# Running ten gate products inside the attention of a kernel's last two layers, with fused bias and maximum

## What is computed

```python
n = rms_norm(h, norm_g[i, 1])
(aq, ak, av, bq, ..., cq, ck, cv, ga, gb, gc) = split_cols(n @ w_in[i], IN_SPLITS)
ya = diff_attention(...)      # 4 heads x 2 parts, causal
yb = nsa_attention(...)       # 8 heads x 3 branches (compressed, selected, window)
yc = swa_sink_attention(...)  # 8 heads, softmax with a sink
merged = (jax.nn.sigmoid(ga) * (ya @ w_branch[i, 0])
          + jax.nn.sigmoid(gb) * (yb @ w_branch[i, 1])
          + jax.nn.sigmoid(gc) * (yc @ w_branch[i, 2]))
h = h + merged @ w_out[i]
```

## Time and profile before

| | us |
|---|---|
| median of three runs | 4402.25 |
| the profiled execution | 4387.95 |
| its span in the trace | 4386.1 |
| attention stage, layer 0 and 1 | 85 and 85 |
| gates stage, layer 0 and 1 | 74 and 73 |

### The profile page before, as it was taken

The page is one execution under the profiler, slowest core; times in us unless marked ns, Lnnn a source line. Parts: engine busy times, 40 slices in busy tenths (PEclk is TensorE's granted clock), DMA queues, the critical chain, the costliest instruction groups (busy, mean ns, idle before and its releaser), DMA issues. The chain is left out here.

```text
span 4386.1 us, 74092 instructions
## 1 busy us (share of the span) xinstructions
PE 4025.2 (92%) x28216; PEld 3843.6 (88%) x28216; DVE 3287.4 (75%) x5784; ACT 2041.9 (47%) x3503; POOL 1184.7 (27%) x1023
## 2 busy tenths in 40 slices
PE   7887988999999998979999999799899989989898
PEld 5666988999999997669999999698788989978897
DVE  6886898778688887668977788666667676667766
ACT  5253334767433334345444444444654454456444
POOL 0000002667688892110188455000000000000000
PEclk9998999999999998989999999899999999989999
DMA  7332445998999995346866888454244545433453
GB/s 254 105 131 101 143 154 181 330 333 293 318 337 333 333 334 193 136 142 204 276 226 217 280 297 300 156 185 162 68 133 161 186 153 186 162 101 101 161 185 124
DMA packets 281605, 896.15 MB, mean 204 GB/s; under 512 B 29424, under 2 KB 73424, under 8 KB 278822
## 3 DMA queue, kind: packets, MB, share of 16 engines
q1 hardware_dynamic: 223286, 673.80, 45.6%
q0 software_dynamic: 55520, 201.60, 13.6%
q10 hardware_dynamic: 2448, 16.02, 0.9%
HBM read 834.92 MB, written 56.14 MB: 203 GB/s over the span
## 5 line engine op out<-in xcount | busy, mean ns | idle before, releaser
L153 DVE TENSOR_TENSOR weight_lo<-weight_ring,weight_hi 128x1024 fp32r<-128x1024 f32 x1084 | 1356.7, 1252 | 633.5 <-ACT weight_hi L148 617.0
L148 ACT ACTIVATE weight_hi<-weight_ring 128x1024 fp32r<-128x1024 f32 x1084 | 1142.6, 1054 | 1210.9 <-issue 706.8
L185 PE MATMUL pair0e_acc<-pair_xh,weight_hi 128*128 128x384 f32 (+1 forms) x1152 | 407.9, 354 | 12.6 <-ACT pair0e_gelu L2679 10.6
L185 PE MATMUL pair0e_acc<-pair_xl,weight_hi 128*128 128x384 f32 (+1 forms) x1152 | 397.0, 345 | 0.0
L185 PE MATMUL pair0e_acc<-pair_xh,weight_lo 128*128 128x384 f32 (+1 forms) x1152 | 396.4, 344 | 0.0
L185 PE MATMUL pair0e_acc<-pair0e_coef_hi,weight_hi 128*128 128x384 f32 x1024 | 343.2, 335 | 9.5 <-DVE pair0e_coef_lo L2391 9.5
L185 PE MATMUL pair0e_acc<-pair0e_coef_lo,weight_hi 128*128 128x384 f32 x1024 | 342.9, 335 | 0.0
L185 PE MATMUL pair0e_acc<-pair0e_coef_hi,weight_lo 128*128 128x384 f32 x1024 | 342.8, 335 | 0.0
L185 PE MATMUL peer10e_dot<-peer_xh,weight_hi 128*128 128x224 f32 (+1 forms) x1152 | 324.8, 282 | 8.2 <-DVE weight_lo L153 6.6
L185 PE MATMUL peer10e_dot<-peer_xh,weight_lo 128*128 128x224 f32 (+1 forms) x1152 | 317.5, 276 | 0.0
L185 PE MATMUL peer10e_dot<-peer_xl,weight_hi 128*128 128x224 f32 (+1 forms) x1152 | 317.4, 276 | 0.0
(11 more groups left out here) (632 smaller groups left out, 12367.1 us busy)
## 6 DMA issues: line engine op xcount, KB each, us to landing
weight_ring<-in_w_tiles SPq DMA_DIRECT2D x572, 512.0 KB
weight_ring<-in_peer_tiles SPq DMA_DIRECT2D x512, 512.0 KB
pair_acts<-pair0e_gelu SPq DMA_DIRECT2D x64, 384.0 KB
pair0e_act_in<-pair_acts SPq DMA_DIRECT2D x64, 384.0 KB
peer_acts<-peer10e_gelu SPq DMA_DIRECT2D x64, 224.0 KB
peer10e_act_in<-peer_acts SPq DMA_DIRECT2D x64, 224.0 KB
pair_coefs<-pair0e_G ACTq DMA_DIRECT2D x12, 1024.0 KB, 14.1
pair0e_kept_in<-pair_coefs SPq DMA_DIRECT2D x64, 192.0 KB
```

What stands on the lines that cost most here:

```text
L148: act.activation(self.tile_of(self.hi, g), self.ring[:, g % RING, :], ACT.Copy).then_inc(self.hi_done, 2)
L153: dve.tensor_tensor(self.tile_of(self.lo, g), self.ring[:, g % RING, :], self.tile_of(self.hi, g).bitcast(F32), ALU.subtract).then_inc(sel ...
L185: last = pe.matmul(out, lhsT, rhs, start=start and i == 0, stop=stop and i == len(passes) - 1, **more)
```

## The change

Of the 24 gate tiles the first ten (`GATES_IN`) are now used inside attention, by a new function `biased_attention` that replaces `attention` in the second block. `GateJobs` does half a tile in each of the 20 steps, on PE behind the scores. All ten use one PSUM bank, `gate_acc`; VectorE scales its sum into `sig` in every second step. ScalarE and VectorE convert the weight tiles there too. The gates stage does the other 14, and ScalarE does the sigmoids of the first ten in it as well. On VectorE the bias and the maximum become one `tensor_tensor_reduce`, which scales by 1/8 after the addition, so the bias table is made 8 times as large. The four results of a step share one PSUM bank: PE waits before a step's first output matmul for all earlier results to be copied, and ScalarE waits for the whole step before it copies them. `sig` now exists during attention; the memory of X_hi and X_lo, not needed by then, lies over it.

```diff
+GATES_IN = 10
...
-            ("ffn1_", 3 * FC), ("in_cols", 21), ("in_rows", 8), ("cmp", 9), ("gates", 24), ("branch", 12),
+            ("ffn1_", 3 * FC), ("in_cols", 21), ("in_rows", 8), ("cmp", 9), ("gates_in", GATES_IN), ("gates", 24 - GATES_IN), ("branch", 12),
...
-        act.activation(self.at(c), self.at(c), ACT.Sigmoid)
+        act.activation(self.at(self.done + c), self.at(self.done + c), ACT.Sigmoid)
+        if c < self.done:
+            act.activation(self.at(c), self.at(c), ACT.Sigmoid)
...
+class GateJobs:
+
+
+    def __init__(self, W, first, x, sig, by_token):
+        self.W, self.first, self.x, self.sig, self.by_token = W, first, x, sig, by_token
+
+    def open(self, S):
+        self.acc = S.ps("gate_acc", [P, 512])
+        self.read = S.sem("gate_read")
+        self.owed = self.W.take_owed()
+        self.kept = 2 * (self.first + GATES_IN) - 1
+        self.W.owed = self.kept
+
+    def feed(self, sync):
+        self.W.feed(sync, self.first, GATES_IN)
+
+    def half(self, pe, n):
+
+        c, half = divmod(n, 2)
+        if c >= GATES_IN:
+            return
+        part = 2 * self.first + n
+        self.W.wait(pe, part)
+        if half == 0 and c:
+            pe.wait_ge(self.read, c)
+        for i in range(4):
+            k = 4 * half + i
+            last = run_passes(pe, self.acc[:, 0:T], self.W.stationary(part, i * P, self.x(k)), k == 0, k == KD - 1)
+        last.then_inc(self.W.used, 1)
+
+    def scale(self, dve, c):
+        if 0 <= c < GATES_IN:
+            dve.wait_ge(self.W.used, 2 * (self.first + c) + 2)
+            dve.tensor_tensor(self.sig[:, c // 8, c % 8, :], self.acc[:, 0:T], self.by_token, ALU.mult).then_inc(self.read, 1)
+
+    def high(self, act, c):
+        if 0 <= c < GATES_IN - 1:
+            self.W.next_hi(act, 2 * (self.first + c) + 1)
+
+    def low(self, dve, c):
+        if 0 <= c < GATES_IN - 1:
+            self.W.next_lo(dve, 2 * (self.first + c) + 1)
...
+def biased_attention(nc, name, units, ident, fill):
...
+        out = S.ps("out", [P, 4, P])
...
+            scores(0)
+            for s in range(steps + 2):
+                scores(s + 1)
+                fill.half(pe, s)
+                for u, i, x in batch(s - 1):
+                    pe.wait_ge(normed, u + 1)
+                    if i % H == 0 and s >= 2:
+                        pe.wait_ge(copied, u - B + H)
+                    for b in range(x.nk // P):
+                        last = pe.transpose(turned[:, i, b * P:(b + 1) * P], prob[:, (s - 1) % 2, i, b * P:(b + 1) * P], ident)
+                    last.then_inc(transposed, 1)
+                for u, i, x in batch(s - 2):
+                    pe.wait_ge(copied, u + 1)
+                    if i == 0 and ends_before(s - 2):
+                        pe.wait_ge(evacuated, ends_before(s - 2))
+                    nb = x.nk // P
+                    for b in range(nb):
+                        last = pe.matmul(out[:, group[u] % 4, :], x.v(b), probT[:, s % 2, i, b * P:(b + 1) * P],
+                                         start=(x.first and b == 0), stop=(x.end and b == nb - 1), skip_group_check=True)
+                    last.then_inc(summed, 1)
...
+            if fill.owed is not None:
+                fill.W.next_lo(dve, fill.owed)
+            for s in range(steps + 1):
+
+                now, b = batch(s), s % 2
+                if now:
+                    dve.wait_ge(scored, s + 1)
+                    for u, i, x in now:
+                        last = dve.tensor_tensor_reduce(biased[:, b, i, 0:x.nk], raw[:, b, place(i), 0:x.nk], x.bias,
+                                                        x.scale, NEG, ALU.add, ALU.max, low[:, b, i:i + 1])
+                    chain(last)
...
+                if s % 2:
+                    fill.scale(dve, (s - 3) // 2)
...
+                if s % 2:
+                    fill.low(dve, (s - 3) // 2)
+            for c in range((steps - 1) // 2, GATES_IN):
+                fill.scale(dve, c)
+                fill.low(dve, c)
...
+                if s % 2:
+                    fill.high(act, (s - 3) // 2)
...
+                done = batch(s - 2)
+                if done:
+                    act.wait_ge(summed, (s - 1) * B)
+                for u, i, x in done:
+                    if x.end:
+                        lo, hi, dst = x.out
+                        act.activation(dst, out[lo:hi, group[u] % 4, :], ACT.Copy).then_inc(evacuated, 1)
...
-                act.activation(bias[:, 2 * n:2 * n + 2, :], acc[:, n % 4, :, :], ACT.Copy).then_inc(copied, 1)
+                act.activation(bias[:, 2 * n:2 * n + 2, :], acc[:, n % 4, :, :], ACT.Copy, scale=8.0).then_inc(copied, 1)
...
-                attention(nc, "attn", units, ident)
+                biased_attention(nc, "attn", units, ident, GateJobs(W, W.take("gates_in" + n), x, sig, in_rstd[:, 0:T]))
...
-            products(nc, W, "gates", first, 24, column_jobs(W, first, 24, KD, T, x),
-                     lambda dve, chain, c, ps: dve.tensor_tensor(sig[:, c // 8, c % 8, :], ps[:, 0:T], in_rstd[:, 0:T], ALU.mult),
-                     "vector", follow=Sigmoids(lambda c: sig[:, c // 8, c % 8, :],
+            def gate(c):
+                return sig[:, c // 8, c % 8, :]
+
+            products(nc, W, "gates", first, 24 - GATES_IN, column_jobs(W, first, 24 - GATES_IN, KD, T, x),
+                     lambda dve, chain, c, ps: dve.tensor_tensor(gate(GATES_IN + c), ps[:, 0:T], in_rstd[:, 0:T], ALU.mult),
+                     "vector", follow=Sigmoids(gate, GATES_IN,
```

More of the change, by code:

```diff
@@ L786, with __init__ @@
 class Sigmoids(Follow):
-    def __init__(self, at, more):
-        self.at, self.more = at, more
+    def __init__(self, at, done, more):
+        self.at, self.done, self.more = at, done, more
     def open(self, S, ready):
@@ L3576, in second_layer @@
             y = tmp_sb("y", [P, 3, 4, T])
+            sig_at = -(-nc.sbuf_base // 32) * 32
+            sig = tmp_sb("sig", [P, 3, KD, T])
             with ExitStack() as attn:
@@ L3582, in second_layer @@
                 X = at_sb("X", [P, 2, 3, XT])
-                X_hi, X_lo = at_sb("X_hi", [P, 11, XT], F32R), at_sb("X_lo", [P, 11, XT], F32R)
+                X_hi, X_lo = (nc.alloc_sbuf_tensor_at("second%d_X_%s" % (layer, part), [P, 11, XT], F32R,
+                                                      offset=sig_at + i * 4 * 11 * XT) for i, part in enumerate(("hi", "lo")))
                 av = at_sb("av", [P, 2, 512])
@@ L3655, in second_layer @@
                                 out=(64 * g, 64 * g + 64, y[half, 2, r, tt * P:(tt + 1) * P])))
-                attention(nc, "attn", units, ident)
+                biased_attention(nc, "attn", units, ident, GateJobs(W, W.take("gates_in" + n), x, sig, in_rstd[:, 0:T]))
             at = col_at("subln") + layer
             y_hi, y_lo = tmp_sb("y_hi", [P, 3, 4, T], F32R), tmp_sb("y_lo", [P, 3, 4, T], F32R)
-            sig = tmp_sb("sig", [P, 3, KD, T])
             term = tmp_sb("term", [P, 2, T])
             first = W.take("gates" + n)
-            products(nc, W, "gates", first, 24, column_jobs(W, first, 24, KD, T, x),
-                     lambda dve, chain, c, ps: dve.tensor_tensor(sig[:, c // 8, c % 8, :], ps[:, 0:T], in_rstd[:, 0:T], ALU.mult),
-                     "vector", follow=Sigmoids(lambda c: sig[:, c // 8, c % 8, :],
+            def gate(c):
[3 more added lines that the diff above has]
+                     "vector", follow=Sigmoids(gate, GATES_IN,
                                                HeadNorm(y, y_hi, y_lo, ones, cols[:, at:at + 1],
@@ L3853, in layout_weights @@
         f["cmp" + n] = np.concatenate([w1, padded_tile(w2)])
-        f["gates" + n] = column_tiles(w[:, 3608:])
+        gate_tiles = column_tiles(w[:, 3608:])
+        f["gates_in" + n], f["gates" + n] = gate_tiles[:GATES_IN], gate_tiles[GATES_IN:]
         wb = a["w_branch_2"][i]
```

87 lines of the change are left out of this document (added).

## The result

The changed kernel takes 4438.42 us (median of five runs, 4428.3 to 4442.33), the kernel before 4407.09 in five runs beside it. The ratio is 1.0086, with an interval of 1.0067 to 1.0105: **slower by 0.9%**. The prediction had +24 us and the right sign. The time lies inside its range, above its middle.

A forecast was written before the change was run, and what follows sets the result against it. PE was taken to become attention's bound: 68.6 + 30.4 + 19 + 6 = 124.0 us against 84.5, +39.5; gates -27.4; net +12.1 a layer, +24 for two. Forecast 4426 us (+0.55%), range 4396 to 4450.

The forecast's parts named there:

- point 7: Start and end of attention: 6 us a layer for the start, its lower clock and the end.
- a rival of 12%: Attention: PE's clock drops again and again behind its pauses, 15 us a layer, 4456 us in all; chance 12%.
- PE's own work: Attention on PE without waits: 68.6 us a layer, plus 30.4 for the half products, 99.0 in all.
- Points 1 and 5: Gates stage loses ten tiles, gain 27.4 us a layer; ScalarE's added weight and copy work in attention priced at 0.
- the first rival: Attention: gate-bank waits cost next to nothing and matmul forms change for free, 94.6 us a layer, 4368 in all; chance 14%.
- Point 3: Attention, single gate bank: PE waits nine times a layer for VectorE's read, 19 us, with 0.9 more in each sink step.
- Point 4: Fused bias and maximum on VectorE: 0.21 us at 128 columns, 0.34 at 256; its saving worthless except inside gate-bank waits.
- The third rival: Attention on VectorE: the fused form takes 0.29 us instead of 0.21, 4 us a layer, 4434 in all; chance 16%.
- Point 6: Attention, one bank for a step's four results: removes PE waits of 1.1 us.
- The sign's turning point: The whole change turns from faster to slower where attention lasts 112 us, nine waits of 1.0 us on top of 103.

The follow-up runs named there:

- read_first: Changed kernel with VectorE's read of the gate bank moved ahead of its wait for the step's scores; 4375.6 us, ratio 0.9963 to the kernel before.
- busy_wait: Changed kernel with 14 extra matmuls, results unused, on PE ahead of each of the nine gate-bank waits; 4414.2 us, ratio 1.0035 to the kernel before.
- only_fused: Changed kernel with no gate tiles in attention, keeping the fused bias and maximum and the single result bank; 4373.15 us, ratio 0.9952 to the kernel before.
- unfused: Changed kernel with bias and maximum as two separate instructions again and the old bias table; 4488.1 us, ratio 1.0205 to the kernel before.
- fused_two_banks: Kernel before with only the fused bias and maximum added, results still in two banks; 4384.89 us, ratio 0.997 to the kernel before.
- half_last: Changed kernel with the half product behind its step's transposes and output matmuls; 4380.27 us, ratio 0.9966 to the kernel before.
- read_first_unfused: Changed kernel with the gate read moved to the front and bias and maximum as two instructions; 4395.2 us, ratio 0.9995 to the kernel before.
- read_last: Changed kernel with VectorE's gate read moved behind the scalings of its step; 4468.87 us, ratio 1.017 to the kernel before.
- busy_7: Changed kernel with 7 extra matmuls on PE ahead of each of the nine gate-bank waits; 4412.28 us in one run.
- busy_3: Changed kernel with three extra matmuls on PE ahead of each of the nine gate-bank waits; 4423.41 us in one run.

## Why the prediction was right in its sign and too small

| us a layer | predicted | measured |
|---|---|---|
| PE without waits, start included | 105.0 | 103.1 (read_first, 1.5 of it waits) |
| nine waits for the gate bank | 19 | 16.7 (busy_wait less read_first) |
| the clock behind those waits | 0 | 12.9 (changed less busy_wait) |
| attention | 124.0 | 132.7 |
| gates | -27.4 | -27.4 |
| branch | 0 | +1.5, +1.4 |
| attention before | 84.5 | 85.6, 86.8 |
| net | +12.1 | +21.1, +20.1 |

**The step that failed is point 7**, "I give 6 us to the start, its clock and the end". It let the clock cost something at the start of the stage alone, and put its return at each wait into a rival of 12%. For the start and the end alone the 6 was enough: read_first has 4.1 us over the 99.0 of PE's own work. The rival had the mechanism ("PE now pauses for about 2 us in every 11"), the place and nearly the price: 15 us a layer against 12.9, though its time, 4456, was 18 us too high. Its test, "if the clock in it is under 0.85", was badly worked out. 15 us lost are 30 us at 1.2 GHz, which over a stage of 139 us with its start make a mean of some 0.87; the measured stage has 0.88, and 27 us of its last 120.6 were low. So by the mark that I set the rival fails, and by the mechanism it held. I gave it so little because one stretch with PE busy for 3.16 of 4 us kept 1.00. But the earlier trace rows also showed 0.64 behind a pause of 0.97 us, and nine pauses of twice that length should have counted for more than one stretch that did not drop. The Trainium skill, TensorE: Matmul & The Clock Gate, section on psum-queue depth-cycling, speaks of micro-idles that make the clock swing; the trace agrees, with 0.57 to 1.00 from one stretch of 4 us to the next.

Point by point for the rest:

- **Points 1 and 5** held: 46.6 us of gates (45 to 47 expected), and no wait of PE for a weight.
- **PE's own work** (68.6 us, and 30.4 for the half products) held twice. only_fused, where PE is the bound, took 75.5 us against 68.6 + 6; read_first took 103.1 against 105.0. The forms at 0.1 us a change are part of both sums, so the first rival, without them and with 94.6 us, fell.
- **Point 3** held: 2.04 us each and 18.4 a layer against 2.1 and 19. The two waits in steps with a sink are the longest, 2.73 and 2.82 us against 1.64 to 1.92 for the others, so the 0.9 more for each is there too. Its mechanism (the read stands behind instructions that wait for the very scores just issued) is shown by read_first, which moves that one instruction: with a single bank, 1.5 us of waits in layer 0 are left. By the rule of the Trainium skill that the prediction named (Perfetto Trace Analysis, section Matmuls) a second bank would do this; the run shows that the order does it too, with no second bank. A second bank was not tried.
- **Point 4** held in its price, 0.21 and 0.34 us from start to start. The third rival, 0.29, fell. "The saving of DVE is therefore worth nothing, except inside the waits" held too: in unfused each wait is 1.6 us longer.
- **Point 6** named waits of 1.1 us a layer that the single bank removes, but took nothing for them in the sum. By only_fused and fused_two_banks it is worth 1.2 and 0.8 us.
- **Branch** was not in the sum. PE's first 4 us there had a granted clock of 0.61 after the change and 1.00 in read_first: (1 - 0.61) x 4 = 1.6 us. Why it falls at that boundary in the changed kernel, half_last and unfused, and not in read_first, is open. In read_first_unfused it fell in layer 1 alone (0.62, a stage of 41.9 us, against 1.00 and 40.7 in layer 0), so a kernel's code doesn't settle it. The stretches, of the changed kernel and of read_first:

```profile
3310.80:3314.80 4.00, 3.96 (x22) 3.99 (x23) 1.65 (x2) 1.06 (x1) 0.00 (x0) 0.61 0.76 281
3272.10:3276.10 4.00, 3.99 (x34) 4.00 (x35) 1.99 (x3) 1.88 (x2) 0.00 (x0) 1.00 0.79 281
```

- **The sign's turning point**, 112 us of attention, was met: read_first_unfused with 112.4 has a ratio of 0.9995.

The sums of the prediction follow from its rows but for small slips: at 0.11 us apart, 112 transposes and 224 output matmuls are 12.3 and 24.6 us, not 12.7 and 24.9, which changes the total by 0.7 us a layer.

Two errors went against each other: the terms without the clock were 4 us a layer too high, and the clock's 12.9 were missing. The kernel without the clock's loss, busy_wait, was at 1.0035, which is a measured +15 us against the predicted +24.

What I had not asked is whether the two parts of the change could both pay. The fused form with the single result bank, and no gate products inside, is faster by 0.5%. It leaves PE as the bound, so the gate products then have no idle time to use: with them, and with the read in the right place, the ratio is 0.9963, and its interval overlaps with that of only_fused, 0.9952. As it was made, the order of one read turned that into +0.9%.

What stays open is what in PE's work around a pause decides whether the clock falls. Longer pauses at the same places cost more (read_last against the changed kernel), but the length of a single one doesn't decide: in the kernel before, the clock fell behind 0.97 us and stayed at 1.00 behind two pauses of 0.97 and 0.98 us that ended at 3162.84 and 3167.60, while in busy_7 it stayed at 1.00 behind 1.70. The extra matmuls changed pause and load at once, so their shares are not separated. Also, busy_7 and busy_3 are single runs; their attention stages agree between the two layers to 0.4 us.

## What to carry to other kernels

Before work is moved into a stage to fill it, ask which engine bounds that stage after the whole change. Here a cheaper VectorE step made TensorE the bound, and TensorE work moved there bought nothing. When a single PSUM bank is read by an engine with a fixed order, place the read ahead of that engine's next wait for the producer; behind it, the producer waits for a chain that it started itself. And price a repeated pause of TensorE twice: its own length, and what the work behind it loses at 1.2 GHz (here 12.9 us on 16.7).

## What the runs showed of the hardware

The granted clock fell behind quite short pauses in a stage where PE was busy for 110.91 of 132.60 us. Nine pauses a layer of 0.93 us on average cost no clock, of 1.40 us 17 us at 1.2 GHz, of 2.04 us 27 and of 3.44 us 44. The length of a single pause was no sure sign: the clock fell behind 0.97 us in the kernel before and behind 1.27 in busy_3, and stayed at 1.00 behind 1.64 in the changed kernel and behind 1.70 in busy_7. Work that is thrown away, put into a pause, made the kernel faster by 0.5% (a ratio of 1.0035 to the kernel before, against 1.0086), since it kept the clock up. In busy_7 it was enough to fill about half of each pause.
